# Two norms of a backbone kernel rebuilt: four wide products and a Newton step for each head, and silu rows spread by TensorE

## The reference

```
sc = silu(c);  sc_ctx = silu(c_ctx)
sh1, sc1, g1, sh2, sc2, g2 = split(sc @ ada_w[i] + ada_b[i], 6)      # and the same from sc_ctx for the context
h = rmsnorm(x) * (1 + sc1) + sh1
q, k, v, g = split(h @ w_in)                                          # 4 heads, q and k 256 wide, v and g 512 wide
o = retention(q, k, v)                                                # forward and backward in time
o = o * rsqrt(mean(o * o, over the head's 512 columns) + 1e-6)        # the heads' norm
y = (silu(g) * o) @ w_out
```

## Time and profile before

| | |
|---|---|
| time, median of 3 runs | 1992.3 us (1991.31 to 1993.33) |
| the profiled execution: time, span | 1993.16 us, 1991.3 us |
| PE busy | 1965.0 us (99% of the span) |
| DVE, ACT busy | 1285.4 us (65%), 721.1 us (36%) |
| mean granted clock of TensorE | 0.997 |
| HBM traffic | 93 GB/s over the span |

### The profile page before, as it was taken

The page is one execution under the profiler, slowest core; times in us unless marked ns, Lnnn a source line. Parts: engine busy times, 40 slices in busy tenths (PEclk is TensorE's granted clock), DMA queues, the critical chain, the costliest instruction groups (busy, mean ns, idle before and its releaser), DMA issues.

```text
span 1991.3 us, 29082 instructions
## 1 busy us (share of the span) xinstructions
PE 1965.0 (99%) x10646; PEld 1686.2 (85%) x10646; DVE 1285.4 (65%) x1961; ACT 721.1 (36%) x1126; POOL 93.0 (5%) x161
## 2 busy tenths in 40 slices
PE   9999999999999999999999999999999999999998
PEld 8888888888888888888888888888888778888886
DVE  7865645735645677765665467867777777467376
ACT  5433224223313343312331233465665543233243
POOL 0000000000000000000000000121111000000000
PEclk9999999999999999999999999999999999999999
DMA  7321311321222122233224323331111222223223
GB/s 306 104 85 64 106 64 54 106 74 55 84 95 64 53 64 95 95 118 116 95 94 127 116 95 119 121 111 49 53 50 47 106 85 95 95 95 105 85 95 106
DMA packets 51268, 186.56 MB, mean 94 GB/s; under 512 B 5680, under 2 KB 5680, under 8 KB 51184
## 3 DMA queue, kind: packets, MB, share of 16 engines
q1 hardware_dynamic: 37744, 136.73, 20.7%
q0 software_dynamic: 13440, 48.63, 7.6%
HBM read 181.15 MB, written 4.19 MB: 93 GB/s over the span
## 4 chain that ended last, share of the span: by engine, by line
PE 95%; DVE 2%; ACT 1%; DMA 1%; issue 1%; SPq 0%; DVEq 0%; POOLq 0%; ACTq 0%
PE acc L404 60%; PE acc L724 6%; PE o_ps L543 4%; PE acc L664 4%; PE o_ps L574 3%; PE acc L543 3%; PE acc L503 2%; PE o_ps L724 2%; PE acc L561 2%; PE acc L759 2%; PE o_ps L710 1%; PE o_ps L689 1%; PE acc L697 1%; DMA ada_start<-in_ada_first_dram 1%; PE o_ps L455 1%
## 5 line engine op out<-in xcount | busy, mean ns | idle before, releaser
L883 ACT ACTIVATE w_hi<-raw 128x1024 fp32r<-128x1024 f32 x223 | 235.8, 1058 | 582.2 <-PE acc L404 466.2
L404 PE MATMUL acc<-h_hi,w_hi 128*128 128x512 f32 x1520 | 434.2, 349 | 3.4 <-ACT u L1095 1.8
L1325 DVE TENSOR_TENSOR w_lo<-raw,w_hi 128x1024 fp32r<-128x1024 f32 x223 | 272.9, 1224 | 253.1 <-ACT w_hi L883 251.6
L404 PE MATMUL acc<-h_lo,w_hi 128*128 128x512 f32 x1520 | 434.9, 349 | 0.0
L404 PE MATMUL acc<-h_hi,w_lo 128*128 128x512 f32 x1520 | 433.7, 348 | 0.0
L404 PEld LDWEIGHTS acc<-h_hi,w_hi 128*128 128x128 f32 x1520 | 243.7, 188 | 43.4 <-ACT u L1095 2.5
L404 PEld LDWEIGHTS acc<-h_hi,w_lo 128*128 128x128 f32 x1520 | 244.5, 188 | 39.3
L404 PEld LDWEIGHTS acc<-h_lo,w_hi 128*128 128x128 f32 x1520 | 243.7, 188 | 38.1
L1490 DVE SCALAR_TENSOR_TENSOR x<-acc,mod,x 128x512 f32<-128x512 f32 (+3 forms) x137 | 82.1, 634 | 149.9 <-PE acc L404 120.9
L404 PE MATMUL acc<-act_hi,w_hi 128*128 128x512 f32 (+1 forms) x396 | 119.9, 356 | 1.3 <-DVE x L1490 1.3
L404 PE MATMUL acc<-act_hi,w_lo 128*128 128x512 f32 (+1 forms) x396 | 120.2, 357 | 0.0
(11 more groups left out here) (263 smaller groups left out, 3388.1 us busy)
## 6 DMA issues: line engine op xcount, KB each, us to landing
raw<-in_weights_dram SPq DMA_DIRECT2D x232, 512.0 KB, 3.4
ada_raw<-in_ada_dram POOLq DMA_DIRECT2D x80, 512.0 KB, 3.7
ada_start<-in_ada_first_dram SPq DMA_DIRECT2D x8, 1024.0 KB, 18.9
x<-in_x_in_dram SPq DMA_DIRECT2D x4, 768.0 KB, 7.1
park_dram<-x POOLq DMA_DIRECT2D x1, 2048.0 KB, 8.1
rel<-in_bias_dram POOLq DMA_DIRECT2D x16, 128.0 KB, 2.4
x<-park_dram POOLq DMA_DIRECT2D x2, 1024.0 KB, 6.8
out_dram<-x SPq DMA_DIRECT2D x8, 256.0 KB, 2.2
```

Source lines behind the costliest of these rows:

```text
L404: mm = nc.tensor.matmul(tile[:, c0:c0 + cn], wt[:, b * P:(b + 1) * P], mv[:, n, c0:c0 + cn], start=(n == 0 and m == 0), stop=(n == last an ...
L883: nc.scalar.activation(w_hi[i][:, :] if spare is None else spare[0], raw[r][:, :], ACT.Copy).then_inc(hi_split, 1)
L1325: nc.vector.tensor_tensor(lo, raw[r][:, :], hi.bitcast(F32), ALU.subtract).then_inc(lo_split, 1)
```

## The change

The silu rows are no longer loaded. PE spreads `silu_c` (the silu of the condition, one column for each feature tile) over all partitions by 16 float32 matmuls against the identity into `acc0` and `acc1`; DVE copies the first to `silu_rows`, ahead of adding squares, and ACT the second, between its second and third square. The 16 idle products on `ident` there give way to these, and 4 stand behind them; 4 more stand behind `token_sums`, and the 3 behind `spread_roots` go. `shift_row(0)` moves behind `spread_roots`.

In each head `token_sums` and `spread_roots` go. ACT and DVE split the summed squares into a high and a low part, and PE multiplies both with `share`, a 128x128 tile of 1/512, in four float32r matmuls (512, 512, 256 and 256 columns) ahead of the second block of project_at(0): the means come out on all partitions at once. ACT takes a first inverse root from its table, and DVE improves it by one Newton step of three instructions. `gated` then reads `ss` and not `spread`. `share` and the split sums lie in the room of `p_hi` and `p_lo`.

```diff
@@ sync @@
-            for c in range(2):
-                sp.dma_start(silu_rows[:, c, :], cond_rows[c, :].partition_broadcast(P)).then_inc(rows_in, 16)
@@ tensor, start @@
-                pe.wait_ge(const_in, 16)
-                idle(16)
+                pe.wait_ge(cond_done, 1)
+                for c in range(2):
+                    for k in range(KC):
+                        mm = nc.tensor.matmul(acc[c][:, k * P:(k + 1) * P], silu_c[:, k, c:c + 1].to_broadcast([P, P]), ident,
+                                              start=True, stop=True)
+                    mm.then_inc(rows_spread, 1)
+                idle(4)
                 for k in range(2, KC):
                     pe.wait_ge(sq_added, k)
                     idle(3)
                 token_sums(KC, TOK)
-                pe.wait_ge(cond_done, 1)
+                idle(4)
+                spread_roots(PARTS)
+                pe.wait_ge(rows_done, 2)
                 shift_row(0)
-                spread_roots(PARTS)
-                idle(3)
                 shift_row(1)
                 shift_row(2)
                 idle(2)
@@ tensor, heads @@
+            def head_means():
+
+                squares_added.up(VC)
+                pe.wait_ge(ss_lo_done, head_squares.up())
+                for c0, cn, _ in PARTS:
+                    for n, z in enumerate((ss_hi, ss_lo)):
+                        mm = nc.tensor.matmul(spread[:, c0:c0 + cn], share, z[:, c0:c0 + cn], start=(n == 0), stop=(n == 1))
+                mm.then_inc(means_done, 1)
...
-                token_sums(VC, TOK)
-                project_at(0, lambda n: spread_roots(PARTS) if n == 3 else None)
+                project_at(0, lambda n: head_means() if n == 1 else None)
                 project_at(1)
@@ scalar @@
                     nc.scalar.activation(S[k % 2][:, 0:width], src[:, k, 0:width], ACT.Square).then_inc(sq_done, 1)
+                    if rows and k == 1:
+                        act.wait_ge(rows_spread, 2)
+                        nc.scalar.activation(silu_rows[:, 1, :], acc[1][:, :], ACT.Copy).then_inc(rows_done, 1)
...
                 squares(vo, VC, TOK)
+                nc.scalar.activation(share, ones[:, :], ACT.Copy, scale=1.0 / RV)
+                act.wait_ge(sq_added, squares_added.now())
+                nc.scalar.activation(ss_hi, ss[:, :], ACT.Copy).then_inc(ss_hi_done, 1)
                 gate(1, *wait_at(1))
-                root(RV, TOK)
+                nc.scalar.activation(nothing[:, :], ones[:, 0:1], ACT.Abs_reciprocal_sqrt)
+                act.wait_ge(means_done, head_squares.up())
+                nc.scalar.activation(S[0][:, 0:TOK], spread[:, 0:TOK], ACT.Abs_reciprocal_sqrt, bias=EPS).then_inc(guessed, 1)
...
-            squares(x, KC, TOK, x_loaded)
-            act.wait_ge(rows_in, 32)
-            nc.scalar.activation(silu_rows[:, :, :], silu_rows[:, :, :], ACT.Silu).then_inc(rows_done, 1)
+            squares(x, KC, TOK, x_loaded, True)
@@ vector @@
+            def split_sums():
+
+                dve.wait_ge(ss_hi_done, head_squares.up())
+                nc.vector.tensor_tensor(ss_lo, ss[:, :], ss_hi.bitcast(F32), ALU.subtract).then_inc(ss_lo_done, 1)
+
+            def one_over_roots():
+
+                mean, first, work = spread[:, 0:TOK], S[0][:, 0:TOK], S[1][:, 0:TOK]
+                dve.wait_ge(guessed, head_squares.now())
+                step(nc.vector.scalar_tensor_tensor(work, mean, EPS, first, ALU.add, ALU.mult))
+                step(nc.vector.scalar_tensor_tensor(work, work, -0.5, first, ALU.mult, ALU.mult))
+                step(nc.vector.scalar_tensor_tensor(ss[:, :], work, 1.5, first, ALU.add, ALU.mult))
...
+                dve.wait_ge(rows_spread, 1)
+                nc.vector.tensor_copy(silu_rows[:, 0, :], acc[0][:, :]).then_inc(rows_done, 1)
                 add_squares(KC, TOK)
-                dve.wait_ge(rows_done, 1)
+                dve.wait_ge(rows_done, 2)
                 scale(0, lambda: one_over(TOK))
...
                 add_squares(VC, TOK)
+                split_sums()
...
-                    step(nc.vector.tensor_tensor(vo[:, g, :], vo[:, g, :], spread[:, 0:TOK], ALU.mult))
+                    step(nc.vector.tensor_tensor(vo[:, g, :], vo[:, g, :], ss[:, :], ALU.mult))
...
-                one_over(TOK)
-                rooted()
+                one_over_roots()
```

More of the change, by code:

```diff
@@ L135, in steps, with backbone @@
         return [(self.full, tiles + extra0), (self.taken[0], tiles // 2 + extra0), (self.taken[1], tiles // 2)]
-def backbone(nc, x_in, weights, ada_first, ada, cond_rows, small_in, bias_in, masks_in, park, out):
+def backbone(nc, x_in, weights, ada_first, ada, small_in, bias_in, masks_in, park, out):
     ctx = ExitStack()
@@ L192, in backbone @@
                 vo = sb("vo", [P, VC, TOK], stack=part)
-                p_hi = [sb(f"p_hi{i}", [P, LAT], F32R, part) for i in range(2)]
-                p_lo = [sb(f"p_lo{i}", [P, LAT], F32R, part) for i in range(2)]
+                p_hi_both, p_lo_both = (sb(f"p_{z}", [P, 2, LAT], F32R, part) for z in ("hi", "lo"))
+                p_hi, p_lo = ([z[:, i, :] for i in range(2)] for z in (p_hi_both, p_lo_both))
+                flat = [z[:, :, :].rearrange("p a t -> p (a t)") for z in (p_hi_both, p_lo_both)]
+                ss_hi, ss_lo = (z[:, 0:TOK] for z in flat)
+                share = flat[1][:, TOK:TOK + P]
                 dist = sb("dist", [P, 896], stack=part)
@@ L240, in backbone @@
         ada_start_in = [sem(f"ada_start_in{k}") for k in range(KC)]
-        rows_in, ada_in, ada_used = sem("rows_in"), sem("ada_in"), sem("ada_used")
+        rows_spread, ada_in, ada_used = sem("rows_spread"), sem("ada_in"), sem("ada_used")
         rows_done, logs_done = sem("rows_done"), sem("logs_done")
@@ L257, in backbone @@
         act_hi_done, act_lo_done = sem("act_hi_done"), sem("act_lo_done")
+        ss_hi_done, ss_lo_done, means_done, guessed = (sem(n) for n in ("ss_hi_done", "ss_lo_done", "means_done", "guessed"))
         rel_in, bias_done, parked = sem("rel_in"), sem("bias_done"), sem("parked")
@@ L371, in _ @@
             squares_added, h_split, p_split, gates_split, act_split = (Tally() for _ in range(5))
-            v_split, qk_split = Tally(), Tally()
+            v_split, qk_split, head_squares = Tally(), Tally(), Tally()
             slot = [0]
@@ L823, in _ @@
             head_attention(True)
-            steps = [(chunk, 16), (diags, 1), (squares_added, VC), (p_split, 7), (v_split, 4), (qk_split, 4), (gates_split, VC)]
+            steps = [(chunk, 16), (squares_added, VC), (head_squares, 1), (p_split, 7), (v_split, 4), (qk_split, 4), (gates_split, VC)]
             with turns(pe, RH - 1, A.steps_at(*HEAD_A) + steps):
@@ L868, in _ @@
             raws, slot, raw_slot = [Tally(), Tally()], [0], [0]
-            roots = Tally()
+            roots, head_squares = Tally(), Tally()
             squares_added, normed, dists, ropes, p_split, value_steps, o_left = (Tally() for _ in range(7))
@@ L894, in wait_after, with squares @@
                 return i, after
-            def squares(src, n, width, loaded=None):
+            def squares(src, n, width, loaded=None, rows=False):
                 for k in range(n):
@@ L1154, in _ @@
             head_attention(True)
-            steps = [(raws[0], 128), (raws[1], 128), (squares_added, VC), (dists, 1), (decays, 4), (ropes, 4), (p_split, 7)]
+            steps = [(raws[0], 128), (raws[1], 128), (head_squares, 1), (squares_added, VC), (dists, 1), (decays, 4), (ropes, 4), (p_split, 7)]
             steps += [(value_steps, 6), (o_left, 1), (gated_chunks, 4), (gates_split, 4), (v_chunks, 3), (v_ends, 1)]
-            with turns(act, RH - 1, A.steps_at(*HEAD_A) + [(roots, 1)] + steps):
+            with turns(act, RH - 1, A.steps_at(*HEAD_A) + steps):
                 head_front(False)
@@ L1769, in _ @@
             head_attention(0, True)
-            steps = [(ada_loads, 128), (hi_splits, 16), (own_steps, 18), (squares_made, VC), (ada_made, 8), (decays, 4)]
+            steps = [(ada_loads, 128), (hi_splits, 16), (own_steps, 21), (head_squares, 1), (squares_made, VC), (ada_made, 8), (decays, 4)]
             steps += [(v_hi_made, TT), (qk_hi_made, 8), (p_hi_made, 7), (gate_hi_made, 4)]
-            with turns(dve, RH - 1, A.steps_at(*HEAD_A) + [(roots, 1)] + steps) as hd:
+            with turns(dve, RH - 1, A.steps_at(*HEAD_A) + steps) as hd:
                 head_front(hd + 1, False)
@@ L2068 @@
     arrays = {"x_in": x_in, "weights": weights, "ada_first": ada_first, "ada": ada[2 * KC:].copy(),
-              "cond_rows": np.stack([a["c"][0], a["c_ctx"]]), "small": np.ascontiguousarray(small),
+              "small": np.ascontiguousarray(small),
               "bias": relative(a["na_rpb"][0]), "masks": mask_tables()}
```

## The result

The changed kernel takes 1983.57 us (median of 5 runs, 1981.89 to 1983.64) against 1992.62 us (5 runs, 1991.31 to 1993.33) for the kernel before in the same comparison: a ratio of 0.995, 95% interval 0.9939 to 0.9962. That is 9.05 us less; the forecast was 8.95 less, 1983.4 us.

A forecast was written before the change was run, and what follows sets the result against it. PE, busy 99% of the span, was taken as the bound; heads 7.45 us plus start 1.5 us made 8.95 us, from the median of 1992.3 to 1983.4 us, range 1980.5 to 1988.

The forecast's parts named there:

- A head's PE work: Each head on PE: removing sums and spreading, adding four matmuls of 0.70 us, saves 1.95 us, bounds 1.82 to 2.02.
- change of kind: In each head on PE: switching between float32 and float32r matmuls costs about 0.1 us more at each of two places.
- rival (d): Heads: change of kind not saved, or wide products pay for changing weights; each head gives 1.5, time 1985.2; chance 0.1.
- Wait for the low part: Each head: DVE's low part of the sums is ready before PE wants it, with 1.6 us of slack.
- Rival (b): Every head waits for the low part of the sums; at 1 us late the time is 1987.4; chance 0.08.
- The Newton step: Each head: ACT's guess 0.81 us, DVE's three instructions 2.97; gated result 1.0 us later, hidden in heads 0 to 2.
- Rival (c): Heads: guess and DVE's steps are dear; 4.4 us longer eats the whole saving, 5 us gives 1994.7; chance 0.04.
- Head 3: Last head, no cover: PE waits 0.9 us ahead of the output projection; it gives 1.6 us instead of 1.95.
- Start, the additions: Start, DVE's additions of squares: the copies of the silu rows delay their end from 15.37 to 18.5 us.
- Start, the shift rows: Start on PE: four shift rows at 1.9 us each, first product of values near 30.6 instead of 32.12, 1.5 us gained.
- Start, the clock: Start on PE: granted clock 1.0 from 17 to 32 us, despite a new pause of about 1.3 us.
- Rival (a): The start gives nothing: clock falls in the new pause or additions end later than 18.5; 1984.9 or 1986; chance 0.22.

## Why the prediction was right, step by step

- **A head's PE work.** Predicted 1.95 us, bounds 1.82 to 2.02; measured 2.00 where nothing else varies: from head 0 to head 1 it is 162.51 or 162.52 us in all nine kernels with the new norm and no longer chain, 164.50 or 164.51 with the old one. The four products take the 0.70 us forecast. Of the two parts of the credit, 2.52 us and 0.1 to 0.2 for the change of kind, the second must be nearly 0.2, so rival (d) is out: the wide products pay no change of kind either.
- **Wait for the low part.** Predicted slack 1.6 us, measured 1.5; no wait in any head. Rival (b) needed another order on ACT, and the run with it lost 10.1 us of waits.
- **The Newton step.** Guess 0.81 predicted, 0.79 measured; three dependent instructions, the gated result 1.1 us later (18.39 us behind the head's row, 654.15 - 636.90 = 17.25 before) where 1.0 was forecast. Hidden in heads 0 to 2, shown by doubling it (0.2 us) and by leaving it out (nothing). Rival (c) was weighed with 2.9 us of slack at the weight split behind the Newton step. That split is in fact the one for the product behind the third gate, not for the third gate as the rival says; the slack is right: 3 us more reached it in head 0 by 0.2. The clock behind a long wait was missing from that rival: 3 us more cost 0.19 + 4.55 = 4.7 us in heads 0 and 3 where its formula has 3.3, so the limit at which the change would turn slower is probably under its 4.4 us; no run was made there.
- **Head 3.** Predicted 1.6 us, a wait of 0.9 ahead of the output projection and none in its middle. Measured 1.75, 0.85, and none. (The prediction lets PE reach the projection behind "four products of about 8.3 us"; they are three, and the time it names, 667.3, is right.)
- **Start, the additions.** Predicted end 18.5, measured 18.98: the copies took 1.22 and 1.02 us as taken (1.2, 1.0), but the spreading they wait for began at 7.14 where I had 6.4, and ACT's came at 10.92 where I had 10.4. The 1.22 us are for 1024 float32 columns from PSUM on DVE; the Trainium skill ("VectorE: DVE Perf Modes", on why PSUM operands drop a tier) gives one element a cycle for it, an estimate of 1.1 us, and the trace agrees within 0.15.
- **Start, the shift rows.** This is the term that was mis-sized: I took each of the four at its duration, 1.9 us, 7.6 together. From 22.71 to 28.01 and from 28.51 to 30.22 they take 7.0, the first alone 24.44 - 22.71 = 1.73; what counts is the distance to the next start. The idle products between took 0.5 where I had 0.6, the steps from the sums to the first shift row 0.2 less. These 0.9 us and the late additions (0.5) nearly cancel: first product at 30.22 where 30.6 was forecast, 1.9 us gained in this pair instead of 1.5, and 1.6 over all profiles.
- **Start, the clock.** It stayed at 1.00 from 17 to 32 us, as forecast, through the pauses between the idle products, the longest of which the profile shows as 0.24 and 0.77 us where one of 1.3 was forecast. Rival (a) did not come; the run without idle products shows what it would have cost, 2.7 us. The Trainium skill ("TensorE: Matmul & The Clock Gate", Part 1) has half rate as the resting state, and the runs agree (0.50 behind 8.15 us of idleness); where the limit lies, these runs do not settle, as the last section tells.
- **What was not forecast.** That the start of before itself varies by 1.3 us from one execution to the next, so that a single pair of profiles doesn't size the start's gain. The distances of head 1 and 2 gained 1.84 and 1.76, not 2.00: where the loop over the heads turns, PE has a gap that the view calls "issue", of 0.4 to 1.1 us, whose length differs from kernel to kernel. It was 0.88 and 0.75 us before and 1.04 and 1.00 after, which is the difference. Its cause stays open, and so does that of a piece of 384 matmuls in the same stretch that takes 67.15 to 67.19 or 67.78 us.
- **The sum.** The mechanisms came as forecast, but that the total is met within 0.1 us is partly luck: the heads gave 7.35 us where 7.45 was forecast, the start 1.9 in this pair where 1.5 was, and the start of before by itself moves the difference by more than either error.

## What to carry to other kernels

When one engine is the bound, price a change by the distance of that engine's instructions, not by their duration, and then look for the one queue position on the others that keeps the new work ahead of it: here it was worth 13.7 us, more than the change. Work that makes a sum later can still bring the end forward if it takes transfers out of a full queue and closes an idle stretch of TensorE behind which its clock may fall to half. Where only the last of several repeated stages is exposed, lengthening the hidden chain once and leaving it out once shows how much room each stage has.

## What the runs showed of the hardware that was not expected

The granted clock does not follow from the length of an idle stretch alone. It fell behind idle stretches of 1.65 us (changed heads with the start of before), 2.02 and 2.18 us (the two profiles of the kernel before), 3.83 us (Newton twice) and 8.15 us (no idle products). Of the four waits of 2.53 us in one and the same kernel it fell behind one (a mean of 0.66 from 320 to 324 us) and stayed at 1.00 behind three, and it stayed at 1.00 through 2.60 us in the kernel with the transferred rows. So a wait of some 2 us on TensorE costs its length, and in some executions more. An estimate from the windows (the half-clock stretch times what it was short of 1.00) is 1.7 us behind the wait of 2.53 us and behind the one of 1.65, and 2.9 and 3.4 us in the two profiles of the kernel before.
